# Experts of a mixture-of-experts layer: 128 stationary columns for products of 96 tokens

## What is computed

```python
for e in range(N_EXPERTS):
    act = jax.nn.silu(hf @ w_gate[e]) * (hf @ w_up[e])      # 1024 -> 512, twice
    y = y + combine[:, e:e + 1] * (act @ w_down[e])         # 512 -> 1024
```

## Time and profile before

| | |
|---|---|
| median of 3 runs | 1267.89 us (1265.67 to 1268.67) |
| profiled execution, span from first to last instruction | 1265.0 us |
| its own time | listed by its span alone |
| TensorE busy | 1170.6 us (93%) |
| VectorE, ScalarE, GpSimd busy | 900.7, 673.1, 196.3 us |
| HBM read | 262.05 MB |
| mean granted TensorE clock | 0.970 of full speed |

### The profile page before, as it was taken

How to read it: one execution, slowest core, us unless ns; L and a number is a source line. 1 busy time by engine, 2 the same in 40 slices (tenths; PEclk the granted TensorE clock), 3 DMA queues, 4 the chain that set the end, 5 groups by cost and what they waited for, 6 DMA issues and landing times.

```text
span 1265.0 us, 16898 instructions
## 1 busy us (share of the span) xinstructions
PE 1170.6 (93%) x5788; PEld 896.4 (71%) x5788; DVE 900.7 (71%) x1221; ACT 673.1 (53%) x843; POOL 196.3 (16%) x158
## 2 busy tenths in 40 slices
PE   5999879999899999999978999999979999999996
PEld 4776559878776777777646688887877677777763
DVE  4646658556469888888877247656657988888886
ACT  4335651133338788788743251122435778878772
POOL 1120000000003222222140000000001222222213
PEclk9999999899989999999999999999979999999998
DMA  6231110113399999999970241113259999999976
GB/s 224 92 90 67 67 54 14 68 67 133 107 340 371 389 386 383 382 385 391 374 270 1 71 109 45 67 67 100 100 196 316 376 383 384 389 384 379 383 291 212
DMA packets 129422, 281.75 MB, mean 223 GB/s; under 512 B 18944, under 2 KB 19456, under 8 KB 129360
## 3 DMA queue, kind: packets, MB, share of 16 engines
q1 hardware_dynamic: 119680, 246.98, 53.7%
q0 software_dynamic: 5888, 20.97, 5.3%
q10 hardware_dynamic: 3792, 12.98, 2.6%
HBM read 262.05 MB, written 18.87 MB: 222 GB/s over the span
## 4 chain that ended last, share of the span: by engine, by line
PE 74%; DVE 17%; ACT 4%; issue 3%; POOL 1%; DMA 1%; DVEq 0%; ACTq 0%; SPq 0%
PE PS L1130 21%; PE PS L1132 20%; PE PS L1131 20%; DVE expert_w_low L1848 4%; PE PS L1234 4%; DVE group_low L1636 2%; PE PS L1364 2%; PE PS L1392 1%; PE PS L1169 1%; DVE score_max L1767 1%; PE PS L1344 1%; DVE hT_low L1620 1%; ACT group_high L915 1%; DVE G L1526 1%; DVE h L1603 1%
## 5 line engine op out<-in xcount | busy, mean ns | idle before, releaser
L1848 DVE TENSOR_TENSOR expert_w_low<-expert_w,weight_high 128x1024 fp32r<-128x1024 f32 x338 | 410.0, 1265 | 69.2 <-ACT weight_high L891 57.9
L891 ACT ACTIVATE weight_high<-expert_w 128x1024 fp32r<-128x1024 f32 x384 | 375.1, 1048 | 56.0 <-PE PS L1132 48.3
L1130 PE MATMUL PS<-weight_high,xgT_high 128*96 128x512 f32 x512 | 204.4, 399 | 2.6 <-DVEq L1858 2.6
L1132 PE MATMUL PS<-weight_high,xgT_low 128*96 128x512 f32 x512 | 203.2, 397 | 0.0
L1131 PE MATMUL PS<-expert_w_low,xgT_high 128*96 128x512 f32 x512 | 202.0, 395 | 0.0
L1130 PE MATMUL PS<-group_high,hT_high 128*128 128x512 f32 x416 | 172.4, 414 | 13.5 <-DVEq L1623 9.1
L1132 PE MATMUL PS<-group_high,hT_low 128*128 128x512 f32 x416 | 164.9, 397 | 0.0
L1131 PE MATMUL PS<-group_low,hT_high 128*128 128x512 f32 x416 | 164.6, 396 | 0.0
L1130 PE MATMUL PS<-weight_high,actT_high 128*96 128x512 f32 x256 | 103.4, 404 | 8.7 <-DVEq L1906 8.5
L1636 DVE TENSOR_TENSOR group_low<-group_w,group_high 128x1024 fp32r<-128x1024 f32 x68 | 80.8, 1222 | 42.9 <-ACT group_high L915 39.4
L1130 PEld LDWEIGHTS PS<-weight_high,xgT_high 128*96 128x96 f32 x512 | 83.3, 163 | 36.0 <-DVEq L1858 2.7
(11 more groups left out here) (252 smaller groups left out, 1520.7 us busy)
## 6 DMA issues: line engine op xcount, KB each, us to landing
expert_w<-in_moe_w_gate SPq DMA_DIRECT2D x32, 2048.0 KB, 14.1
expert_w<-in_moe_w_up SPq DMA_DIRECT2D x32, 2048.0 KB, 16.0
expert_w<-in_moe_w_down SPq DMA_DIRECT2D x32, 2048.0 KB, 15.0
group_w<-in_even_w_in SPq DMA_DIRECT2D x6, 2048.0 KB, 7.8
group_w<-in_odd_w_in SPq DMA_DIRECT2D x6, 2048.0 KB, 7.9
y_rows<-yb ACTq DMA_DIRECT2D x30, 384.0 KB, 6.1
group_w<-in_even_w_out SPq DMA_DIRECT2D x2, 2048.0 KB, 7.7
h_rows<-h SPq DMA_DIRECT2D x8, 512.0 KB, 10.9
```

Of the source, the lines that this page charges most:

```text
L891: act_(hi, w, ACT.Copy).then_inc(w_hi, 1)
L1130: pe.matmul(out, ah, bh, start=first, stop=False)
L1132: return pe.matmul(out, al, bh, start=False, stop=final)
L1848: tt(lo, w, hi.bitcast(F32), ALU.subtract).then_inc(w_lo, 1)
```

## The change

Each expert product gets a stationary operand of 128 columns: its own 96, and the 32 behind them in SBUF, which are the first of the next chunk. The product then writes 128 partitions of its PSUM bank, of which 96 to 127 are read by nobody. The last chunk of gate and up (k = 7) has no chunk behind it and keeps 96 columns; it is multiplied before chunk 6, so that the last product of an accumulation is a wide one. For down, the tiles `actTh` and `actTl` get 32 more columns, which are filled once per layer with a constant (two copies on ScalarE), so all four chunks are wide. `actTl` starts 128 bytes later for that.

```diff
-        actTh = sb("actT_high", [P, DE // P, CAP], F32R)
-        actTl = sb("actT_low", [P, DE // P, CAP], F32R)
+        ACT_N = DE // P * CAP
+        actTh = sb("actT_high", [P, DE // P * CAP + P - CAP], F32R)
+        actTl = sb("actT_low", [P, DE // P * CAP + P - CAP], F32R)
...
+                if l == 0:
+                    sc.wait_ge(consts, 11)
+                for a in (actTh, actTl):
+                    act_(a[:, ACT_N:], iota_f[:, 0:P - CAP], ACT.Copy)
                 rows_T(0, 0)
...
-                    for k in range(KD):
-                        if k % KS == 0:
-                            wait_low(p0, b0, k // KS)
-                        if k == KD // 2 and midway:
+                    for n, k in enumerate((*range(KD - 2), KD - 1, KD - 2)):
+                        if n % KS == 0:
+                            wait_low(p0, b0, n // KS)
+                        if n == KD // 2 and midway:
                             midway()
-                        ins = three(bank(key)[0:CAP], ((xgTh[:, par, k], xgTl[:, par, k]),
-                                                       (hi[:, k], lo[:, k])), k == 0, k == KD - 1)
+                        wide = P if k < KD - 1 else CAP
+                        rows = [a[:, par].rearrange("p k n -> p (k n)")[:, k * CAP:k * CAP + wide] for a in (xgTh, xgTl)]
+                        ins = three(bank(key)[0:wide], (rows, (hi[:, k], lo[:, k])), n == 0, n == KD - 1)
...
+                        rows = [a[:, k * CAP:k * CAP + P] for a in (actTh, actTl)]
                         for c in range(2):
-                            ins = three(PS[0:CAP, 2 + c], ((actTh[:, k], actTl[:, k]),
-                                                           (hi[:, 2 * k + c], lo[:, 2 * k + c])),
+                            ins = three(PS[:, 2 + c], (rows, (hi[:, 2 * k + c], lo[:, 2 * k + c])),
                                         k == 0, k == DE // P - 1)
```

More of the change, by code:

```diff
@@ L1059, in block_act @@
                     bk.wait_full(sc, key, b)
-                    act_(actTh[:].rearrange("p k n -> p (k n)"), bank(key)[:, 0:4 * CAP], ACT.Copy
+                    act_(actTh[:, 0:ACT_N], bank(key)[:, 0:4 * CAP], ACT.Copy
                          ).then_inc(actTh_ready, 1)
@@ L1903, in block_ve @@
                     ve.wait_ge(actTh_ready, b + (l * NE + 1))
-                    link(tt(actTl[:].rearrange("p k n -> p (k n)"), bank(key)[:, 0:4 * CAP],
-                            actTh[:].rearrange("p k n -> p (k n)").bitcast(F32), ALU.subtract))
+                    link(tt(actTl[:, 0:ACT_N], bank(key)[:, 0:4 * CAP], actTh[:, 0:ACT_N].bitcast(F32), ALU.subtract))
                     ve.sem_inc(actT_ready, 1)
```

## The result

The changed kernel takes 1273.49 us, median of 14 runs (1270.90 to 1276.21); the kernel before, in the same series on the same chip, 1267.98 us, median of 14 runs (1264.01 to 1271.78). The ratio is 1.0045, 95% interval 1.0033 to 1.0058: slower by 5.5 us (4.2 to 7.4 by the interval). I had forecast 1262.4 us, faster, and a range up to 1272.5. Three executions further down, one of s512_w96 and two of s512_w128_fill, were disturbed and took 1885 to 3019 us; their ratios leave them out.

What follows compares the result with a forecast made beforehand. TensorE was taken as the bound: in expert stages, product count times pitch. A pitch gain of 6.3 to 8.8 us less 1.9 for exposed loads, taken as 5.5, gave 1267.9 - 5.5 = 1262.4 us; range 1258.5 to 1272.5.

Steps and rivals of the forecast that it cites:

- item 4: Expert gate, up and down: pitch falls from 232.0 towards 226.7 ns, gaining 6.3 to 8.8 us over 32 expert sets.
- the step of the address: Rival, 30%: the expert chunks' 384-byte step, not width, prevents the quick pitch; it stays 232.0 ns, 1269.8 us.
- none at 226.7 is a loss of 1.9: Lower bound on the pitch gain: no expert product reaches 226.7 ns, leaving only the exposed weight loads' 1.9 us.
- 3 points: Share of the 30% address-step case counted as slower, where the pitch at the new addresses is worse.
- Item 3: First products after transposes, some 62 places: wider weight loads in the open cost about 0.03 us each, +1.9 us.
- Item 2: Within product streams: loads grow from 163 to 192 ns but stay under the previous product, costing nothing.
- Items 5, 6 and 7: Gate/up chunk swap, two ScalarE copies per layer (about 0.5 us, covered) and the unchanged 384-column `actT_low` subtraction: each costs nothing.
- The rival of the width switches: Rival, 17%: the narrow gate/up chunk's 128 width changes cost 50 to 90 ns each, 6.4 to 11.5 us.
- Late weights: Rival, 7%: faster products exhaust the 2.6 us of weight-load cover in layer 1, capping the gain: 1265 us.
- lock: Regular 226.7 ns pitch that long 128-column streams find within some ten products and keep; 96-column streams nearly never keep it.

Runs made afterwards that it cites:

- s512_w96: Kernel before with stationary token chunks (xgT, actT) 512 bytes apart instead of 384, still 96 columns: 1267.91 us, ratio 0.9980.
- s512_w128_fill: s512_w128 plus 16, 8 and 8 unread 128x128 products ahead of TensorE's waits in each layer's last two expert blocks: 1266.45 us, ratio 0.9988.
- s512_w128: Kernel before with chunks 512 bytes apart and all 128 columns wide, the extra 32 filled with a constant: 1269.00 us, ratio 0.9997.
- s384_allwide: Changed kernel with chunk 7 also filled to 128 columns, natural order, step still 384 bytes: 1273.64 us against 1268.93, ratio 1.0035.

## Why the prediction was wrong, and where it was right

1. **The step that failed is item 4**, the gain in pitch, 6.3 to 8.8 us. I took 226.7 ns from streams that are 128 wide and step by 2048 bytes, and gave it to streams that step by 384. In the changed kernel 8% of the starts are that quick, where 37 to 52 of an expert's 72 products had been counted on. The two kinds of rows differ in two things, and I put the difference down to one. The runs show that both are needed for a lasting quick pitch: at 384 bytes 128 columns give 231.9 and 233.0 ns, at 512 bytes 96 columns give 230.0, and only 512 bytes with 128 columns give 227.6 and 228.5. What a single chunk can do is another matter: the six products at 226.7 ns in the earlier trace rows had 96 columns and a step of 384 bytes. Such starts are 2% of down's in the kernel before, and no run here explains them. The rival "the step of the address" was right in its outcome and half right in its mechanism: the width counts too, as soon as the step allows it.
2. **That rival's price was too low.** It left the pitch at 232.0 and charged 1.9 us: 1269.8. But down had not been at 232.0: it was at 230.9, of which I had no row, and went to 233.1. The terms as measured: gate and up (232.1 - 231.9) x 1536 products = 0.3 us, down (233.1 - 230.9) x 768 = 1.7 us, and the exposed loads 25 ns x 64 = 1.6 us. That is 3.6 us, and the growth of an expert, 0.12 us x 32, gives 3.8. Measured are 5.5 (4.2 to 7.4). The rest, about 2 us, isn't placed: the runs after spend 81 us at the low clock, those of the kernel before 79 (from the other series; this one lists no clock for it), which is worth 0.7 us. In the profiled executions the changed kernel loses 0.96 + 0.70 = 1.7 us of full-speed work behind a wait in layer 0, where the kernel before loses none, but one execution of each can't place it.
3. **The range** ended 1 us too low for that reason. The bound "none at 226.7 is a loss of 1.9" left room for no gain in pitch, but for no loss either; a layout whose addresses change can also be worse than today's, and I had given that 3 points and no price.
4. **Item 3, exposed loads, was right**: about 0.03 us at each of 62 places, 1.9 us, against 0.025 x 64 = 1.6 us.
5. **Item 2, hidden loads, was right**: 190 to 192 ns at 128 columns. In s512_w128 they lie under a pitch of 226.7 ns and cost nothing.
6. **Items 5, 6 and 7 were right**: the swap doesn't show (17.79 us per expert with it and the narrow chunk, 17.77 without both), the copies have no wait behind them, and VectorE's busy time is 4 us lower than before rather than higher.
7. **The rival of the width switches** is refuted by the rows at 1118.26 and 1118.95 us and by s384_allwide. The Trainium skill, "TensorEngine Tiling (Array Packing)", section Key Properties, has a change of tiling mode drain TensorE; by these rows a change between 96 and 128 columns is no such change.
8. **Late weights** were not reached by the change, which takes them later, not earlier. In s512_w128, which takes them earlier, I read 0.6 to 1.5 us between landing and ScalarE's read for most loads near the end of the stages, where 2.6 us had been the least. The cover is nearly used up and still holds.
9. **What I called a lock** behaves as described once the layout allows it: ten pitches at 231 ns, then 47 at 226.8. What makes it in the chip isn't shown.

The Trainium skill, "TensorE: Matmul & The Clock Gate", section on weight-path perf modes, has fast weight load on at 128 columns of a type that isn't FP32. Measured are 190 ns at 128 columns against 163 at 96, and the exposed loads became a cost. Whatever that rule counts this fp32r form as, nothing quick shows.

## What to carry to other kernels

A pitch read from one stream may be carried to another only if both agree in everything that the operands have: width, step, and where the tile begins. Where two differ, look for rows that have one without the other, and if there are none, make the kernel that has. Here a place of 512 bytes for each chunk is what the idea of the change needed, not 128 columns read over the end of a place of 384; and a gain in the flow of products has to be followed to the stage's end, where a short idle time of TensorE may give part of it back through the clock.

## What the runs showed of the hardware that was not expected

- The pitch of fp32r products of 128x512 at a clock of 1.00 depends on where the stationary operand lies: 226.7 to 233.6 ns for the same 512 streamed columns. In gate and up a step of 512 in place of 384 bytes is worth 2 ns at 96 columns and 4.3 at 128.
- At a step of 384 bytes, wider is not quicker, and in down it is slower (230.9 to 233.1 ns); at 512 bytes each 16 columns more are quicker (230.0, 229.3, 227.6 ns in gate and up). What in the chip makes this is open.
- A shift of 64 bytes at the same step and width cost down 4.8 ns (228.5 to 233.3, one run).
- TensorE's clock fell to 1.2 GHz behind idle times of 1.4 to 2.4 us at the ends of both stages in s512_w128, and in the kernel before, whose idle times there are 1.3 to 2.2 us, only once, at the end of layer 1's. With products without use in those gaps the granted clock stayed at 1.00 there in the profiled executions.
